# Experts' up stage: high and low activations as one 512-column product, the halves added afterwards

## What is computed

```python
def chunk(xc):
    q = (xc @ wq).reshape(PEER_CHUNK, PEER_HEADS, 2, half)
    sc = jnp.einsum('chpd,hpnd->chpn', q, sub_keys)
    s1, i1 = lax.top_k(sc[:, :, 0], PEER_TOPK)
    s2, i2 = lax.top_k(sc[:, :, 1], PEER_TOPK)
    ...
    top_s, pos = lax.top_k(cand, PEER_TOPK)
    g = jax.nn.softmax(top_s, axis=-1)
    u_sel = jnp.take(u, eidx, axis=0)
    a = jax.nn.gelu(jnp.einsum('chkd,cd->chk', u_sel, xc), approximate=False)
    w = (g * a).astype(x.dtype)
    return jnp.einsum('chk,chkd->cd', w, jnp.take(v, eidx, axis=0))
```

## Time and profile before

| | us |
|---|---|
| median of three runs | 2537.97 |
| lowest, highest | 2535.24, 2539.03 |
| profiled execution | 2538.06 |
| its span | 2536.3 |
| TensorE, VectorE, ScalarE, GpSimd busy | 2420.6, 1772.8, 1347.1, 706.5 |
| mean granted clock of TensorE | 0.99 |

### The profile page before, as it was taken

The page is one execution under the profiler, slowest core; times in us unless marked ns, Lnnn a source line. Parts: engine busy times, 40 slices in busy tenths (PEclk is TensorE's granted clock), DMA queues, the critical chain, the costliest instruction groups (busy, mean ns, idle before and its releaser), DMA issues. The chain is left out here.

```text
span 2536.3 us, 57328 instructions
## 1 busy us (share of the span) xinstructions
PE 2420.6 (95%) x16507; PEld 2215.3 (87%) x16507; DVE 1772.8 (70%) x3913; ACT 1347.1 (53%) x2394; POOL 706.5 (28%) x540
## 2 busy tenths in 40 slices
PE   7899999999999999989999999999999988999998
PEld 6789999999888888888999999988888886788996
DVE  5747777787777777564777788777777667555346
ACT  3534555676655555454555567655555533434443
POOL 4665444000000000556544400000000052144665
PEclk9999999999999999999999999999999998899999
DMA  6244666544566666623466644456666634332553
GB/s 238 79 144 153 210 225 214 181 162 170 179 237 246 240 237 245 228 84 137 163 223 222 229 157 162 175 190 236 247 239 238 254 126 149 130 133 99 178 191 147
DMA packets 98051, 475.28 MB, mean 187 GB/s; under 512 B 11808, under 2 KB 13344, under 8 KB 50720
## 3 DMA queue, kind: packets, MB, share of 16 engines
q1 hardware_dynamic: 97392, 472.91, 52.5%
q10 hardware_dynamic: 560, 1.19, 0.1%
HBM read 438.41 MB, written 35.65 MB: 187 GB/s over the span
## 5 line engine op out<-in xcount | busy, mean ns | idle before, releaser
L1366 ACT ACTIVATE wh<-ring 128x512 fp32r<-128x512 f32 x1428 | 882.6, 627 | 624.1 <-ACTq L1365 620.6
L2037 DVE TENSOR_TENSOR wl<-ring,wh 128x512 fp32r<-128x512 f32 x961 | 678.0, 711 | 268.0 <-DVEq L2036 249.2
L1062 PE MATMUL PS<-xh,wh 128*128 128x256 f32 x2048 | 593.1, 290 | 10.7 <-PEq L1058 8.8
L1062 PE MATMUL PS<-xl,wh 128*128 128x256 f32 x2048 | 578.9, 283 | 0.0
L1062 PE MATMUL PS<-xh,wl 128*128 128x256 f32 x2048 | 578.8, 283 | 0.0
L504 POOL TENSOR_TENSOR wl<-ring,wh 128x512 fp32r<-128x512 f32 x295 | 392.0, 1351 | 298.5 <-POOLq L503 294.9
L865 PE MATMUL PS<-wh,xh 128*128 128x512 f32 x1088 | 425.1, 391 | 2.9 <-PEq L862 2.7
L865 PE MATMUL PS<-wh,xl 128*128 128x512 f32 x1088 | 423.4, 389 | 0.0
L865 PE MATMUL PS<-wl,xh 128*128 128x512 f32 x1088 | 423.3, 389 | 0.0
L1062 PEld LDWEIGHTS PS<-xh,wh 128*128 128x128 f32 x2048 | 391.7, 191 | 17.9 <-issue 17.3
L1062 PEld LDWEIGHTS PS<-xl,wh 128*128 128x128 f32 x2048 | 392.3, 192 | 0.0
(11 more groups left out here) (334 smaller groups left out, 3856.2 us busy)
## 6 DMA issues: line engine op xcount, KB each, us to landing
ring<-in_peer_u SPq DMA_DIRECT2D x128, 1024.0 KB, 4.8
ring<-in_peer_v SPq DMA_DIRECT2D x128, 1024.0 KB, 4.8
acts<-stg SPq DMA_DIRECT2D x124, 256.0 KB, 2.0
gains<-acts SPq DMA_DIRECT2D x124, 256.0 KB, 4.9
ring<-in_w_in SPq DMA_DIRECT2D x24, 1024.0 KB, 4.9
ring<-in_w_gate_up SPq DMA_DIRECT2D x22, 1024.0 KB, 4.8
ring<-in_peer_wq SPq DMA_DIRECT2D x16, 1024.0 KB, 4.8
ring<-in_w_down SPq DMA_DIRECT2D x11, 1024.0 KB, 4.8
```

The costliest lines, as they stand in the source:

```text
L1062: last = pe.matmul(PS[:, 2 * j, 0:S], w[:, q, k * P:(k + 1) * P], x[:, at, :], start=at + i == 0, stop=at + i == 9)
L1366: act.activation(wh[:, q, :], ring[:, s, q * QW:(q + 1) * QW], ACT.Copy).then_inc(high_ready[q], 1)
L2037: part = dve.tensor_tensor(wl[:, q, :], ring[:, s, q * QW:(q + 1) * QW], wh[:, q, :].bitcast(F32), SUB)
```

## The change

- `xh` and `xl` become two halves of one tile `xhl`, so that the high and low part of a block's 256 tokens lie side by side.
- For each block TensorE issues one product of `wh` by 512 columns (high and low activations) and one of `wl` by 256 columns, which is accumulated onto the first 256. Each half of a chunk now fills a bank of its own, and the banks alternate between chunks (`2 * j + odd`).
- ScalarE copies the second 256 columns to `stg` (`second_sum`), VectorE adds the first 256 from PSUM (`summed`), and ScalarE applies Gelu in place (`expert`), for half 1 a chunk later.
- In routing a sum stands behind each low part of VectorE.
- From chunk 39 on GpSimd makes the low parts of quarters 0 to 2, VectorE that of quarter 3.
- On SyncE's queue the load of the next chunk stands ahead of the store of the activations.

```diff
@@ TensorE @@
-                                for i, (w, x) in enumerate(((wh, xh), (wh, xl), (wl, xh))):
-                                    last = pe.matmul(PS[:, 2 * j, 0:S], w[:, q, k * P:(k + 1) * P], x[:, at, :],
-                                                     start=at + i == 0, stop=at + i == 9)
+                                pe.matmul(PS[:, 2 * j + odd, :], wh[:, q, k * P:(k + 1) * P],
+                                          xhl[:, at, :, :].rearrange("p i n -> p (i n)"), start=at == 0, stop=False)
+                                last = pe.matmul(PS[:, 2 * j + odd, 0:S], wl[:, q, k * P:(k + 1) * P], xh[:, at, :],
+                                                 start=False, stop=at == 7)
@@ ScalarE @@
+                def second_sum(odd, j, first=False):
...
+                    act.activation(stg[:, odd, j * S:(j + 1) * S], PS[:, 2 * j + odd, S:2 * S],
+                                   ACT.Copy).then_inc(dve_full[j], 1)
+
+                def expert(s, j, kept=False):
+
+                    act.wait_ge(sum_ready[j], 1)
+                    act.sem_inc(sum_ready[j], -1)
+                    act.sem_inc(slot_free[j], 1)
+                    half = stg[:, s, j * S:(j + 1) * S]
+                    last = act.activation(half, half, ACT.Gelu)
...
                     high(s, 0)
-                    expert(c - 1, 1 - s, 0, first)
+                    second_sum(1 - s, 0, first or unsaved)
                     high(s, 1)
+                    if not first:
+                        expert(s, 1)
                     if slots:
                         gates_out(at, slots[0])
                     high(s, 2)
                     if len(slots) > 2:
                         gates_out(at + 4, slots[1])
-                    expert(c - 1, 1 - s, 1, kept=kept)
+                    second_sum(1 - s, 1)
                     high(s, 3)
+                    expert(1 - s, 0)
@@ VectorE @@
+                def summed(odd, j):
+
+                    dve.wait_ge(dve_full[j], 1)
+                    dve.sem_inc(dve_full[j], -1)
+                    half = stg[:, odd, j * S:(j + 1) * S]
+                    dve.tensor_tensor(half, PS[:, 2 * j + odd, 0:S], half, ADD).then_inc(sum_ready[j], 1)
...
                 def low_odd(k):
                     low(k // 2 % 2, 2 * (k % 2) + 1)
+                    summed(1 - k // 2 % 2, k % 2)
...
                 def lows(s, at, slots):
 
-                    low(s, 0, 2)
-                    low(s, 1, 2)
+                    summed(1 - s, 0)
                     onehots(at, slots[0])
-                    low(s, 2, 2)
                     if len(slots) > 2:
                         onehots(at + 4, slots[1])
-                    low(s, 3, 2)
+                    low(s, 3)
+                    summed(1 - s, 1)
                     onehots(at + 4 * len(slots) - 4, slots[-1])
@@ GpSimd @@
                 pool.sem_inc(dve_lows_done, -1)
+                low_rest(NPAIR - N_GATE)
+                pool.sem_inc(pool_lows_done, 1)
+                pool.wait_ge(dve_lows_done, 1)
+                pool.sem_inc(dve_lows_done, -1)
@@ SyncE @@
                 with sp.Fori(0, NPAIR // 2 - 2) as i:
+                    load_u(2 * i + 3, 1)
                     save_acts(2 * i, 0)
-                    load_u(2 * i + 3, 1)
+                    load_u(2 * i + 4, 0)
                     save_acts(2 * i + 1, 1)
-                    load_u(2 * i + 4, 0)
```

More of the change, by code:

```diff
@@ L175, in build @@
         pool_lows_done = sem("pool_lows_done")
+        sum_ready = [sem(f"sum_ready{j}") for j in (0, 1)]
         acts_out = [sem(f"acts_out{s}") for s in (0, 1)]
@@ L1049, in _, with experts @@
                 pe.sem_inc(keys_in, -16)
-                def experts(beside=()):
+                def experts(odd, beside=(), first=False):
                     for j in range(2):
                         pe.wait_ge(slot_free[j], 1)
-                        pe.sem_inc(slot_free[j], -1)
+                        if not first:
+                            pe.sem_inc(slot_free[j], -1)
                         for q in (2 * j, 2 * j + 1):
@@ L1081, in gates @@
                     last.then_inc(act_full[2 + s], 1)
-                with pe.Fori(0, N_GATE - 1):
-                    experts()
+                experts(0, first=True)
+                experts(1)
+                with pe.Fori(0, N_ROUTE // 2 - 1):
+                    experts(0)
+                    experts(1)
+                experts(0)
                 pe.wait_ge(src_ready, 1)
@@ L1090, in _ @@
                                [(ps2(2 + t)[:, i * P:(i + 1) * P], sel[:, i, t, :]) for i in range(3)])
-                experts()
+                experts(1)
                 with pe.Fori(0, 6):
[L1094 to L1097, removed]
+                    experts(0, (0, 1, 0))
+                    experts(1, (1, 0, 1))
+                with pe.Fori(0, 7):
+                    experts(0, (0, 1))
+                    experts(1, (0, 1))
+                for j in range(2):
+                    pe.wait_ge(slot_free[j], 2)
+                    pe.sem_inc(slot_free[j], -1)
                 for s in (2, 3):
@@ L1614, in gates_out @@
                                    ACT.Copy).then_inc(slot_free[2 + s], 1)
-                experts(1, 1, True)
-                experts(2, 0, True)
-                with act.Fori(1, N_ROUTE // 2) as i:
-                    experts(2 * i + 1, 1)
-                    experts(2 * i + 2, 0)
+                experts(1, True)
+                experts(0, unsaved=True)
+                with act.Fori(1, N_ROUTE // 2):
+                    experts(1)
+                    experts(0)
                 act.wait_ge(smarg_ready, 1)
@@ L2338, in low_odd, with low_first @@
                     low(k // 2 % 2, 2 * (k % 2) + 1)
+                    summed(1 - k // 2 % 2, k % 2)
+                def low_first(k):
+                    if k < 2:
+                        low(0, 2 * k + 1)
+                    else:
+                        low_odd(k)
                 dve.wait_ge(pool_lows_done, 1)
                 dve.sem_inc(pool_lows_done, -1)
-                best_keys(N_WQ - 2, 0, low_odd)
+                best_keys(N_WQ - 2, 0, low_first)
                 best_keys(N_WQ - 1, 1, low_odd)
@@ L2408, in _, with low_and_sum @@
                 dve.sem_inc(pool_lows_done, -1)
+                def low_and_sum(s, q):
+                    low(s, q, 2)
+                    if q % 2:
+                        summed(1 - s, q // 2)
                 for q in range(4):
-                    low(0, q, 2)
+                    low_and_sum(0, q)
                 dve.wait_ge(smexp_ready, 1)
@@ L2463, in _ @@
                 lows(1, S - 8, (0, 1))
+                for j in range(2):
+                    summed(1, j)
                 for s in (0, 1):
```

51 lines of the change are left out of this document (27 added, 24 removed).

## The result

| | before | after |
|---|---|---|
| median us (4 runs each) | 2537.59 | 2627.82 |
| lowest, highest | 2535.24, 2539.03 | 2627.44, 2628.45 |
| ratio of the medians, 95% interval | | 1.0358, 1.0343 to 1.0373 |
| profiled execution's span | 2536.3 | 2625.5 |

A forecast was written before the change was run, and what follows sets the result against it. VectorE and TensorE were taken as tied within 2% in routing, VectorE the longer chain; TensorE bounds the gates' part. Terms 48 + 2 + 26 + 9 - 1.3 + 1 + 1.5 = +86 us give 2624; range 2562 to 2682.

The forecast's parts named there:

- ScalarE is seen waiting for the sums: One of three signs that would prove the prediction wrong; ScalarE's copies and waits were taken as hidden.
- follows a low part that is already out: ScalarE's new wait, half 0: the sum's preceding low part is already issued, so the next high part isn't delayed.
- The 27 us: TensorE's merged products: 0.21 us less a chunk, 27 us over 128 chunks if TensorE set the pace everywhere.
- Sums: VectorE in routing: eight sums add 2.5 us a turn; six ahead of the loop add +2 in all.
- Hold-ups in routing: GpSimd's low parts hold VectorE up about 2.9 us a turn before; the shifted phase adds 0.5.
- Gates' part: GpSimd's low parts hold up one-hots, making VectorE the bound: chunks of 9.5 and 7.9 us, +26 and +9.
- Rival B: Gates' part: GpSimd's low parts fall into VectorE's slack, TensorE keeps the pace; +41, 2579 us; chance 0.13.
- Hand-over: Ahead of the first one-hots: one more sum and a drain, +1 us for both layers.
- the forecast of the clock: Routing: TensorE keeps full clock, as stretches of idle stay around a microsecond.
- SyncE's order: Load ahead of store costs nothing: the store lands in 2.0 us, the buffer's next copy over half a chunk off.
- three chunks: Chunks between the routing and gates' parts run at TensorE's pace: -0.21 x 6 = -1.3 us.
- the tail: Last sums and Gelus behind the last product: +1.5 us.

The follow-up runs named there:

- the last experiment: Kernel before with merged products from chunk 38 on, chunks of three and two groups in turn, store ahead of load in routing: 2535.8 us, ratio 0.9987.
- all three cuts: Kernel after with all sums left out and GpSimd's low parts in routing and gates' part cut to 8 of 512 columns: 2514.08 us, ratio 0.9901.

## Why the prediction was right, and where it was not

**What bounds it.** Right for the kernel after: work put on VectorE lengthened the routing turns by about its own length, and TensorE's late starts are mostly ahead of VectorE's quarters. For the kernel before it is shown that the turns were not at TensorE's pace (23.04 with GpSimd's instructions short); that VectorE was the one is argued, and quarter 0, which waits for the ring's load, ScalarE and GpSimd, had its part in it.

**The signs.** The prediction named as a sign of being wrong that ScalarE is seen waiting for the sums. It is, 38.4 us over six turns of layer 0. The step behind it (the sum "follows a low part that is already out") was wrong as a statement on ScalarE, which runs ahead of VectorE and idled ahead of its high parts and Gelus before too. It did not show in VectorE's chain, whose waits for high parts stay at 0.3 us or less; whether it has a part in the 6.3 us ahead of quarter 0 isn't separated. GpSimd is busy 41% in the gates' part, not 50%. TensorE's idle share of a turn, 14% and 10%, and the full clock in routing are near the forecast.

**TensorE: mis-sized.** 0.21 us a chunk was forecast; within a quarter blocks do stand 0.35 apart in the gates' part after (504.79, 505.14, 505.49, 505.83) against 0.36 before, but a chunk gained 0.17 there, and 0.13 in routing. The 27 us are 13 to 16 with everything else out of the way in both kernels. In the kernel after nearly none of it shows, so the forecast hardly rests on it.

**Sums.** Forecast 2.5 a turn and 2 ahead of the loop, 42 in all; leaving them out took 42.0 away. By the turns it is 2.8 and 1.7 in the two layers, 2.3 on average, so the exact match is luck. The last of a turn went as forecast: the gap at the loop's head fell from 0.93 to 0.21.

**Hold-ups in routing.** Forecast 3.4 a turn where 2.9 were before; making GpSimd's low parts small took 3.4. The turns of 25.9 and 27.1 lie on either side of the forecast 26.5. That layer 0 has three stretched low parts and layer 1 two, from the same code, is what the range's bounds were for.

**Gates' part.** Three groups: 9.48 against 9.5. The mechanism is the forecast's, but two terms are off and cancel: the holds are 2.46 us in the chunk shown (0.96, 0.50 and 1.00) and about 2.5 in the others, not 2.85, and VectorE's chain without them is 7.0, not 6.66, with a gap of 0.22 ahead of the second one-hots. Two groups: mostly 7.6 to 7.8 against 7.9, 7.53 before, +0.12 on average instead of +0.35. That is 29 us instead of 35; why the holds cost less there I didn't look into. 31.4 were measured, with some 3 of the clock's loss in it. Rival B falls: the holds don't go into slack. Making GpSimd's low parts small there takes 42.6 us away, more than these 29, as TensorE's own saving then shows and the hand-over is shorter.

**Hand-over: mis-sized.** Forecast +1. Measured are 2.3 and 1.9 us more of TensorE's idle time, and 4.9 us lost at half clock, 9 us together. The step counted the sum and the drain ahead of the one-hots and left out that GpSimd's first low parts, moved to the same instant, hold these one-hots; the forecast of the clock looked only at routing, where it stayed full.

**SyncE's order: wrong.** The prediction costed it at nothing, since the buffer was needed half a chunk later. It asked when the store has to be done and not what it does to the load beside it. In the kernel before the order costs 16 us. In the kernel after, the load lands in 5.0 and the store in 3.7. VectorE's chain is the longer one there and may hide a part; but TensorE is late ahead of quarter 0 by 6.3 us, as with the load first in the kernel before (5.9), and not by the 2.6 of before. How much of the 90 us it is stays open: the store first was not tried in the kernel after. If it costs anything there, the routing terms above hold it, and their sum is right in spite of a missing term.

**What made the total fit.** Routing +54.7 against 50 forecast (sums, hold-ups, three chunks, hand-over), gates +31.4 against 36.5 with the tail, the rest +3.1 against 0, which no experiment explains. The two large mechanisms, sums on VectorE's chain and holds by GpSimd, are shown. That the total is within 4 us is in part luck: the hand-over and the rest cost 11 us more than forecast, and the chunks of the gates' part 6 less.

## What to carry to other kernels

Ask for each stage which engine has no long wait, not which is busiest: here a saving of 13 us on an engine at 95% came with a loss of 90, since the work went to the one whose short waits only looked like slack. Giving VectorE's work to an idle GpSimd is no gift where their instructions read SBUF at once: three low parts of 0.60 us given away cost VectorE 2.5 us in holds in a chunk of three groups, and moving them back saved 39 us. And a DMA moved in a queue is costed by what else is in flight when it starts, not only by when it has to be done.

## What the runs showed of the hardware

Two transfers issued 0.6 us apart, 1 MB in and 256 KB out, landed in 5.2 us each (medians of all in that kernel 5.3); a pair 2.8 us apart took 4.8 and 2.6.

A VectorE sum with one operand in PSUM ran beside GpSimd's low parts 137 times without taking over 426 ns; four tensor_scalars of 128x128, 1.11 us alone, took 2.07 beside one low part and 3.06 where they met two.

TensorE's clock at the hand-over did not go by the idle time that the trace shows. In the profiled execution of the kernel before it stayed full behind 2.35 and 2.72 us idle, and fell to 0.5 behind 2.35 us in the kernel before with small low parts and behind 2.39 in the last experiment. With all three cuts made, one execution has 2.34 us of idle in both layers, and the clock fell in layer 0 and stayed full in layer 1. What decides between them I could not tell from these traces; keeping TensorE at work through the wait kept it full in both layers. As each kernel was profiled in one execution, a few us between two profiled spans can be this alone.
